# Finding the picked row and column keys in a product-key expert layer: sixteen equality tests on 2-byte values in place of three fp32 passes

## The reference

```
q  = (x @ w_pq).reshape(T, 8, 2, 128)
sc = einsum('thpc,hpkc->thpk', q, sub_keys)      # 2 x 128 scores per token and head
sv, si = top_k(sc, 16)                           # 16 best row keys and 16 best column keys
cand = sv[..., 0, :, None] + sv[..., 1, None, :]
cid  = si[..., 0, :, None] * 128 + si[..., 1, None, :]
fv, fi = top_k(cand, 16)                         # 16 best pairs
eid  = take_along_axis(cid, fi)                  # expert = (row key, column key)
g    = softmax(fv)
out  = sum over picks of g * gelu(u_experts[eid] . x) * v_experts[eid]
```

## Time and profile before

| | us |
|---|---|
| median of 3 runs | 2184.36 (2181.97 to 2188.09) |
| the profiled execution, its own time | 2184.32 |
| its span, first to last instruction | 2182.7 |
| PE busy | 2127.6 |
| DVE busy | 1580.2 |
| ACT busy | 1098.5 |
| POOL busy | 343.3 |

### The profile page before, as it was taken

How to read it: one execution, slowest core, us unless ns; L and a number is a source line. 1 busy time by engine, 2 the same in 40 slices (tenths; PEclk the granted TensorE clock), 3 DMA queues, 4 the chain that set the end, 5 groups by cost and what they waited for, 6 DMA issues and landing times. The chain is left out here.

```text
span 2182.7 us, 47685 instructions
## 1 busy us (share of the span) xinstructions
PE 2127.6 (97%) x15224; PEld 1975.6 (91%) x15224; DVE 1580.2 (72%) x2591; ACT 1098.5 (50%) x1651; POOL 343.3 (16%) x344
## 2 busy tenths in 40 slices
PE   6999999999999999999989999999999999999998
PEld 6999899999999888888789989999999998888886
DVE  6665658998777676677675746599977776767776
ACT  6445454444455555555464545444455554555554
POOL 3110110000000143344230101100000003333331
PEclk9999999999999999999999999999999999999999
DMA  5444466765555777777634454566655557777775
GB/s 188 156 151 154 146 203 216 228 205 184 182 182 181 244 251 240 241 241 240 225 127 155 148 167 166 185 228 229 201 182 180 180 180 264 242 240 241 241 240 165
DMA packets 173982, 437.49 MB, mean 200 GB/s; under 512 B 19360, under 2 KB 84896, under 8 KB 172752
## 3 DMA queue, kind: packets, MB, share of 16 engines
q1 hardware_dynamic: 173232, 432.09, 60.7%
q0 software_dynamic: 672, 4.39, 0.6%
HBM read 399.70 MB, written 36.70 MB: 200 GB/s over the span
## 5 line engine op out<-in xcount | busy, mean ns | idle before, releaser
L750 DVE TENSOR_TENSOR w_lo<-raw,w_hi 128x1024 fp32r<-128x1024 f32 x680 | 842.1, 1241 | 406.9 <-ACT w_hi L718 193.9
L1152 PE MATMUL ps<-act_hi,w_hi 128*128 128x256 f32 x2880 | 830.6, 288 | 3.2 <-DVE act_lo L801 1.9
L1152 PE MATMUL ps<-act_hi,w_lo 128*128 128x256 f32 x2880 | 816.9, 284 | 0.0
L1152 PE MATMUL ps<-act_lo,w_hi 128*128 128x256 f32 x2880 | 816.2, 283 | 0.0
L1152 PEld LDWEIGHTS ps<-act_hi,w_hi 128*128 128x128 f32 x2880 | 554.1, 192 | 5.2 <-issue 2.3
L1152 PEld LDWEIGHTS ps<-act_hi,w_lo 128*128 128x128 f32 x2880 | 554.5, 193 | 0.1
L1152 PEld LDWEIGHTS ps<-act_lo,w_hi 128*128 128x128 f32 x2880 | 554.3, 192 | 0.0
L718 ACT ACTIVATE w_hi<-raw 128x1024 fp32r<-128x1024 f32 x248 | 263.1, 1061 | 324.0 <-PE ps L1412 311.5
L1412 PE MATMUL ps<-w_hi,act_hi 128*128 128x512 f32 x1000 | 389.2, 389 | 1.8 <-DVE act_lo L1116 1.8
L1412 PE MATMUL ps<-w_lo,act_hi 128*128 128x512 f32 x1000 | 389.0, 389 | 0.0
L1412 PE MATMUL ps<-w_hi,act_lo 128*128 128x512 f32 x1000 | 389.0, 389 | 0.0
(11 more groups left out here) (249 smaller groups left out, 2060.0 us busy)
## 6 DMA issues: line engine op xcount, KB each, us to landing
raw<-slabs SPq DMA_DIRECT2D x684, 512.0 KB, 3.7
h_park<-h_out SPq DMA_DIRECT2D x256, 128.0 KB, 1.7
h_in<-h_park SPq DMA_DIRECT2D x250, 128.0 KB, 3.9
memT<-mem POOLq DMA_DIRECT2D x2, 1024.0 KB, 6.9
skT<-sub_keys POOLq DMA_DIRECT2D x2, 1024.0 KB, 7.1
x_park<-xT SPq DMA_DIRECT2D x2, 1024.0 KB, 5.3
xT<-x_park SPq DMA_DIRECT2D x2, 1024.0 KB, 8.5
xT<-x SPq DMA_DIRECT2D x1, 1024.0 KB, 4.9
```

The costliest lines, as they stand in the source:

```text
L750: nc.vector.tensor_tensor(w_lo[:, j].rearrange("p k c -> p (k c)"), raw[:, j, :], w_hi[:, j].rearrange("p k c -> p (k c)").bitcast(FP32), ...
L1152: last = nc.tensor.matmul(ps[:, j, 0:T], w[:, j, k, :], a[:, k, :], start=(k == 0 and i == 0), stop=(k == KB - 1 and i == 2))
```

## The change

The three fp32 passes over 16 values are replaced for both keys. The row's number in the candidate list is now computed: `by16_u` and `by8_u` are the position shifted right by 4 and 3, and row = max(position/16, position/8 - 2, position - 72), which with the three blocks of `CAND` gives 0 to 15; it is written in bf16 as `a_at`. The column goes to bf16 as `b_at`. Then for each a from 0 to 15 one `scalar_tensor_tensor` over all 256 places computes (place == a) * key[a] into slice a of `pick`, which is now bf16 and 16 slices of 256; the key operand stays fp32 and is repeated over the 16 picks. A tree of four additions (8, 4, 2 and 1 slices) sums the 16 slices in bf16; the last one writes `row_f` or `col_f` in fp32. Keys are integers below 128, and of 16 slices 15 are zero. `cand_at` and `top_d` go, the arguments of `spend` are new, and `g_rest` moves to another address.

```
--- before.py
+++ after.py
@@ -177,7 +177,6 @@
         tri = sb("tri", [P, P])
         iota = at("iota", top[0], [P, P, 2], BF16)
         top[0] += P * 2 * 2
-        cand_at = sb("cand_at", [P, TOPK])
         par_at = top[0]
         par = sb("par", [P, N_PARAM])
         wif_hi = sb("wif_hi", [P, KB, 8], F32R)
@@ -193,7 +192,7 @@
 
 
         def tmp(name, kib, shape, dt=FP32):
-            size = 4
+            size = 2 if dt == BF16 else 4
             for n in shape[1:]:
                 size *= n
             assert kib * 1024 + size <= NKEYS * T * 4, name
@@ -249,7 +248,11 @@
         top_i = tmp("top_i", 90, [P, TB * SETS, TOPK])
         fin_v = tmp("fin_v", 92, [P, TB * PH, TOPK])
         fin_i = tmp("fin_i", 93, [P, TB * PH, TOPK], U32)
-        top_d = tmp("top_d", 94, [P, TB * PH, TOPK])
+        a_at = tmp("a_at", 94, [P, TB * PH * TOPK], BF16)
+        b_at = tmp("b_at", 94.5, [P, TB * PH * TOPK], BF16)
+        a_f = tmp("a_f", 112, [P, TB * PH * TOPK])
+        by16_u = tmp("by16_u", 113, [P, TB * PH * TOPK], U32)
+        by8_u = tmp("by8_u", 114, [P, TB * PH * TOPK], U32)
         bit_u = tmp("bit_u", 95, [P, TB * PH * TOPK], U32)
         low_u = tmp("low_u", 102, [P, TB * PH * TOPK], U32)
         bit_f = tmp("bit_f", 103, [P, TB * PH * TOPK])
@@ -259,11 +262,11 @@
         col_f = tmp("col_f", 99, [P, TB * PH * TOPK])
         g_exp = tmp("g_exp", 100, [P, TB * PH, TOPK])
         g_sum = tmp("g_sum", 101, [P, TB * PH])
-        pick = tmp("pick", 104, [P, TB * PH * TOPK, TOPK])
+        pick = tmp("pick", 104, [P, TOPK, TB * PH, TOPK], BF16)
         top_u = tmp("top_u", 104, [P, TB * SETS, TOPK], U32)
         cand = tmp("cand", 106, [P, PH, N_CAND])
         struck = tmp("struck", 109, [P, 2, NKEYS])
-        g_rest = tmp("g_rest", 104, [P, T // 2, 2])
+        g_rest = tmp("g_rest", 115, [P, T // 2, 2])
 
         h_park = nc.dram_tensor("h_park", (NKEYS, P, T), FP32, kind="Internal").ap()
         x_park = nc.dram_tensor("x_park", (P, KB, T), FP32, kind="Internal").ap()
@@ -433,11 +436,6 @@
             nc.gpsimd.iota(iota[:], [[1, P], [0, 2]], base=0, channel_multiplier=0,
                            allow_small_or_imprecise_dtypes=True).then_inc(consts, 1)
             pool.dma_start(par[:], params[0]).then_inc(par_loaded, 16)
-            first = 0
-            for a0, na, nb in CAND:
-                nc.gpsimd.iota(cand_at[:, a0:a0 + na], [[nb, na]], base=first, channel_multiplier=0,
-                               allow_small_or_imprecise_dtypes=True).then_inc(consts, 1)
-                first += na * nb
 
             def scale(dst, count, evacs, xns):
 
@@ -813,7 +811,7 @@
                 nc.vector.tensor_tensor(w_lo[:, j].rearrange("p k c -> p (k c)"), raw[:, j, :],
                                         w_hi[:, j].rearrange("p k c -> p (k c)").bitcast(FP32),
                                         ALU.subtract).then_inc(lo_ready[j], 1)
-            dve.wait_ge(consts, 4 + len(CAND))
+            dve.wait_ge(consts, 4)
             with dve.Fori(0, DEPTH) as layer:
 
                 dve.wait_ge(par_loaded, layer * 16 + 16)
@@ -1002,9 +1000,6 @@
                 step.mark(nc.vector.tensor_copy(top_i[:], top_u[:]))
 
                 step.join()
-                rows = top_i[:].rearrange("p (c s) a -> p c s a", s=2)[:, :, 0, :]
-                step.mark(nc.vector.tensor_copy(top_d[:, :, 0:1], rows[:, :, 0:1]))
-                step.mark(nc.vector.tensor_tensor(top_d[:, :, 1:TOPK], rows[:, :, 1:TOPK], rows[:, :, 0:TOPK - 1], ALU.subtract))
                 for b in range(TB):
                     tops = top_v[:, b * SETS:(b + 1) * SETS, :].rearrange("p (h s) a -> p h s a", s=2)
                     step.join()
@@ -1028,41 +1023,38 @@
                 flat_i = fin_i[:].rearrange("p c k -> p (c k)")
                 step.mark(nc.vector.tensor_scalar(bit_u[:], flat_i, 8, None, ALU.bitwise_and))
                 step.mark(nc.vector.tensor_scalar(low_u[:], flat_i, 7, None, ALU.bitwise_and))
+                step.mark(nc.vector.tensor_scalar(by16_u[:], flat_i, 4, None, ALU.logical_shift_right))
+                step.mark(nc.vector.tensor_scalar(by8_u[:], flat_i, 3, None, ALU.logical_shift_right))
                 step.mark(nc.vector.tensor_copy(at_f[:], flat_i))
-                spend(1.3)
+                spend(1.6)
                 step.join()
-
 
 
                 step.mark(nc.vector.scalar_tensor_tensor(bit_f[:], at_f[:], float(CAND[0][1] * CAND[0][2]), bit_u[:],
                                                          ALU.is_lt, ALU.mult))
                 step.mark(nc.vector.scalar_tensor_tensor(b_f[:], at_f[:], float(N_CAND - CAND[2][1]), low_u[:],
                                                          ALU.is_lt, ALU.mult))
+                step.mark(nc.vector.scalar_tensor_tensor(a_f[:], by8_u[:], -2.0, by16_u[:], ALU.add, ALU.max))
                 step.join()
-                step.mark(nc.vector.tensor_tensor(b_f[:], b_f[:], bit_f[:], ALU.add))
-                spend(1.3)
-                cols = top_i[:].rearrange("p (c s) a -> p c s a", s=2)[:, :, 1, :]
-                pick4 = pick[:].rearrange("p (c k) a -> p c k a", k=TOPK)
-                halves = [slice(b * PH * TOPK, (b + 1) * PH * TOPK) for b in range(TB)]
-                for place, marks, test, keys, found in ((at_f, cand_at, ALU.is_ge, top_d, row_f),
-                                                        (b_f, iota[:, :, 0], ALU.is_equal, cols, col_f)):
+                step.mark(nc.vector.tensor_tensor(b_at[:], b_f[:], bit_f[:], ALU.add))
+                step.mark(nc.vector.scalar_tensor_tensor(a_at[:], at_f[:], float(CAND[2][0] - (N_CAND - CAND[2][1])), a_f[:],
+                                                         ALU.add, ALU.max))
+                spend(2.2)
+                keys = top_i[:].rearrange("p (c s) a -> p c s a", s=2)
+                for side, (place, found) in enumerate(((a_at, row_f), (b_at, col_f))):
                     step.join()
-                    for h in halves:
-                        step.mark(nc.vector.tensor_tensor(
-                            pick[:, h], place[:, h].unsqueeze(2).to_broadcast([P, PH * TOPK, TOPK]),
-                            marks[:, 0:TOPK].unsqueeze(1).to_broadcast([P, PH * TOPK, TOPK]), test))
-                        spend(2.3)
-                    step.join()
-                    for b in range(TB):
-                        c = slice(b * PH, (b + 1) * PH)
-                        step.mark(nc.vector.tensor_tensor(
-                            pick4[:, c], pick4[:, c],
-                            keys[:, c, :].unsqueeze(2).to_broadcast([P, PH, TOPK, TOPK]), ALU.mult))
-                        spend(2.3)
-                    step.join()
-                    for h in halves:
-                        step.mark(nc.vector.tensor_reduce(found[:, h], pick[:, h], AX.X, ALU.add))
-                        spend(2.3)
+                    for a in range(TOPK):
+                        step.mark(nc.vector.scalar_tensor_tensor(
+                            pick[:, a], place[:].rearrange("p (c k) -> p c k", k=TOPK), float(a),
+                            keys[:, :, side, a].unsqueeze(2).to_broadcast([P, TB * PH, TOPK]), ALU.is_equal, ALU.mult))
+                        spend(0.45)
+                    n = TOPK // 2
+                    while n:
+                        step.join()
+                        out = found[:].rearrange("p (o c k) -> p o c k", o=1, k=TOPK) if n == 1 else pick[:, 0:n]
+                        step.mark(nc.vector.tensor_tensor(out, pick[:, 0:n], pick[:, n:2 * n], ALU.add))
+                        spend(0.13 * n + 0.2)
+                        n //= 2
                 step.join()
                 dve.wait_ge(gexp_ready, layer + 1)
                 step.link(nc.vector.tensor_reduce(g_sum[:], g_exp[:], AX.X, ALU.add))
```

## The result

| | before | after |
|---|---|---|
| median of 9 runs | 2185.07 us (2181.58 to 2190.14) | 2173.43 us (2170.40 to 2178.82) |
| profiled execution, span | 2182.7 us | 2168.7 us |
| mean granted clock | 0.993 | 0.995 |

The ratio is 0.9945, with a 95% interval of 0.9934 to 0.9955: 11.6 us faster by the medians, 10 to 14 us by the interval. The forecast was 8.0 us, 2176.3 us, with a range from 2173.2. The forecast started from 2184.36 us for the kernel before, which measured 2185.07 here. The direction was right, the gain was 3.6 us larger than forecast.

The account below looks back on a forecast made before the run. PE, busy 2127.6 of 2182.7 us, was taken to bound the kernel. Ending its wait for decoded gains 3.84 us in the first layer and 4.20 in the second, 8.0 off 2184.32: 2176.3 us, range 2173.2 to 2181.2.

Parts of the forecast that it names:

- 3.2 us ahead of PE's request: End of DVE's look-up, first layer: decoded comes at 480.1, 3.2 us before PE asks for it at 483.35.
- Products at 0.34 us: DVE's look-up: 32 products with test over 256 elements start every 0.34 us, 10.88 us in all.
- additions at 1.22 us: DVE's look-up: each tree's first addition, 2048 bf16 elements, takes 1.22 us; two trees take 5.48 us.
- DVE held by ACT: Look-up: DVE waits for ACT's w_hi; 3 us of nearly 10 us of saved work go into these waits.
- The wait that takes the place of the old one: PE at the first gates, behind slabs 58 and 59: waits 1.2 to 1.4 us for hot_row once per layer.
- the chain: DVE from copying the transposes to the first gates: small instructions, w_lo 60 and 61, one-hot tiles; unchanged at 6.76 us.
- The time in hand: DVE in the look-up: decoded is 3.2 us early, and 3 us of saved work go into waits for ACT.
- take 0.74 us of issue: PE's transposes behind slab 57, first layer: start at 483.35, take 0.74 us, so slab 58 starts at 484.09.
- From the first gates on nothing changes: The gates loop behind the look-up: DVE already waits for PE there, 96.5 us in all, so no gain.
- The clock did not drop at the new wait: Rival, chance 0.13: PE's clock drops at the hot_row wait, costing 1.5 to 2.2 us per layer; 2179.3 to 2180.7 us.
- The product was not dear: Rival, chance 0.07: look-up products with repeated fp32 operand cost 0.73 us each, decoded comes 2.5 us later per layer; 2189.4 us.
- nothing would be gained: Rival, chance 0.05: the chain behind the transposes, or ACT, holds PE, so earlier decoded is worth little; 2184 us.

Follow-up runs that it names:

- e3: Changed kernel with DVE's w_lo of slab 60 ahead of its wait for the transposes instead of behind it: 2171.42 us, ratio 0.9945.
- e11: Changed kernel with only the row side's 16 products issued a second time, into a tile nobody reads: 2173.97 us.
- e10: Changed kernel with all 32 products issued a second time, into a tile nobody reads: 2181.93 us.
- e1: Changed kernel with 64 bytes left free where cand_at stood, so tiles above keep their old addresses: 2175.60 us, ratio 0.9960.
- e2: Kernel before, old look-up, with cand_at placed behind all other tiles, giving the new addresses: 2181.53 us, ratio 0.9980.
- e6: Changed kernel with pick in fp32 instead of bf16, so products and tree use 4-byte values: 2173.33 us.
- e7: Kernel before, arithmetic untouched, with w_lo of slabs 58 and 59 moved behind the instruction that raises decoded: 2180.59 us, ratio 0.9979.
- e4: Changed kernel with act_hi and act_lo 32 bytes further up and all tiles above them 128 bytes further: 2174.72 us.
- e5: Changed kernel with act_hi and act_lo 32 bytes up, but the v_experts part given its own tiles at the old address: 2148.61 us, ratio 0.9834.
- e8: Changed kernel with act_hi and act_lo 64 bytes further up and all tiles above them 128 bytes further: 2178.22 us.

## Why the prediction was right and where it was wrong

**Right, step by step.** `decoded` was forecast 3.2 us ahead of PE's request and came 3.35 us ahead. Products at 0.34 us, additions at 1.22 us, DVE held by ACT (3.0 us of waits in the look-up against about 3), the table load ahead of slab 56 as the point that sets the end: all as worked out. The wait that takes the place of the old one was forecast at 1.2 to 1.4 us and is 1.05 us of idle time, or 1.21 us counted as the forecast did, by starts (487.38 + 0.12 to 488.71). From the copy to the first gates the chain takes 6.76 us (481.95 to 488.71), as forecast; e3 shows that it is the chain named. The time in hand, 3.3 us at `decoded` and about 6 us of DVE's work, is confirmed from both sides by e11 and e10. The page "VectorE: DVE Perf Modes" in the Trainium skill (section "The TRN2 errata — SBUF-src ops pay a fixed extra latency per instruction") has small tiles paying their fixed latency each time; here products of 256 elements last 0.42 us but start every 0.34 us. Even 0.08 us more for each of the 32, 2.6 us, would have cost nothing, since e11 adds 5.4 us and loses nothing.

**Mis-sized: the transposes.** The step "take 0.74 us of issue" read them at a granted clock of 0.85 (487.10 to 487.84), behind the pause. At full clock they take 0.58 us (481.09 to 481.67), and the copy starts 0.28 us behind them instead of 0.39. That is 0.27 us per layer: 4.11 and 4.48 us where 3.84 and 4.20 were forecast, 8.6 instead of 8.0. A duration that is read inside the disturbance which a change removes belongs to the disturbance.

**The step that failed: "From the first gates on nothing changes"** and the sum taken over the look-up alone. The prediction put the effect of the change on all other matmuls at nothing. Of `cand_at` it counted only the three iotas that fill it, not the 64 bytes that go from the middle of the allocation. That moved the streamed operands of 1152 matmuls and made each 3.3 ns faster, 3.8 us. e1 and e2 show this with either look-up. 8.6 + 3.8 is 12.4 us, against 11.6 measured (10 to 14 by the interval). The kernel that the prediction added up is really e1, the new look-up with all addresses kept: 0.9960 x 2184.36 is 2175.6 us, against the 2176.3 forecast.

**The rest of the 14.0 us between the two profiled executions**, 1.6 us, is put down to scatter. It stands in the early stages of each layer, where PE waits for norms and the clock falls. The first 96 matmuls take 15.64 us before and 17.93 in the changed kernel, a loss; between 65 and 75 us the clock was 0.50 for 6.8 us before and stayed at 1.00 after, a gain of 3.1 us; the first 96 matmuls behind the norm of the second layer take 13.19 and 11.38 us, a gain. These lengths differ in the same way between kernels that are equal there: the first 96 matmuls take 17.88 us in e3 and 15.72 in e6. Outside the look-up and the end of the program, PE spent 17.1 us at 0.50 before and 13.7 after, which is an estimated 1.7 us. Over the nine runs of the changed kernel the mean granted clock and the time go together, 0.995 at 2170.40 us and 0.992 at 2178.82.

**Rivals.** The clock did not drop at the new wait (1.00 from 488.70 on). e7 shows that this was not safe: behind pauses of 1.44 and 0.34 us it dropped in one layer and not in the other. The product was not dear. That nothing would be gained is refuted.

**What stays open** is why addresses matter. The runs show that the pace of these matmuls changes when one of their two operands is moved by 32 or 64 bytes while the weight slab stays, and that moving the activations speeds the matmuls that stream them and slows those that hold them stationary. Whether the address itself or the distance to the other operand counts was not tried. A move of 128 bytes changes the pace too (`mem_hi` and `mem_lo` in e4), and e5 has two paces for one pair of addresses, so something else has a part in it.

## What to carry to other kernels

When DVE feeds the engine that sets the time and does a side task too, ask when the side task must be done, and what stands ahead of it in program order: here moving two instructions (e7) gave 2.9 us at the look-up, and the full new arithmetic 8.6. Once the side task is done in time, a still cheaper form is worth nothing, as the 2-byte values show (e6). A diff that adds or removes a tile is also a diff of addresses: compare start-to-start times of untouched matmuls in both traces before crediting the code, and try the operands' addresses on purpose.

## What the runs showed of the hardware that was not expected

- fp32r matmuls of 128x256 with the streamed tile at the offsets tried start every 0.120 us (`act_hi`, with `w_hi` at a multiple of 128 bytes and `act_hi` too), 0.1167 us (`act_hi` 32 bytes up, e4) or 0.1176 us (64 bytes up, e8). `pre_hi` went from 0.120 us at 96 bytes past a multiple of 128 to 0.1167 us at 32 bytes past one. The offset is not all: in e5 one stretch ran at 0.1178 us in the first layer and 0.1167 in the second.
- fp32r matmuls of 128x512 with the activations stationary start every 0.2267 us with both operands at multiples of 128 bytes, and every 0.233 us with the stationary one 32 or 64 bytes off.
- A pause of 3.6 us left PE at a granted clock of 0.52 for the next slab; a pause of 1.05 us at the first gates left it at 1.00. Pauses of 1.44 and 0.34 us in a row (e7) were followed by 0.58 over the next 4.1 us in one layer and by 1.00 in the other.
